# Scores and transposes of every second attention step behind the next group of products

## The reference

```
# layer 0: pooling mixer on 768 columns + memory attention (4 heads of 64) on 256
# layer 1: dilated window attention (12 heads: 3 groups, (window, dilation) =
#          (128,1), (512,4), (2048,16)) + memory attention
z = rms_norm(x, g) @ w_in[l]
s = einsum(q, k) * 64**-0.5          # per head; masked to a band for dilated attention
p = exp(s - logsumexp(s))
o = einsum(p, v)
# dilated groups: o weighted by softmax over the groups' logsumexp
x = x + rms_norm(concat(y_main, y_mem) @ w_out[l], g1)
h = rms_norm(x, g2); x = x + rms_norm((silu(h@wg) * (h@wu)) @ w_down[l], g3)
# after layer 0: shared keys and values, kv = rms_norm(x) @ w_kv, rotary on k
```

## Time and profile before

| | before |
|---|---|
| median of 3 runs | 2105.54 us (2105.05 to 2107.71) |
| the profiled execution: time, span | 2110.79 us, 2109.0 us |
| mean granted TensorE clock | 0.985 of full |
| TensorE busy | 2003.6 us, 95% |
| VectorE, ScalarE, GpSimd busy | 1466.9, 938.2, 340.2 us |
| TensorE waiting for ACT before scores (L869) | 32.5 us in 27 waits |
| TensorE waiting before transposes (L880) for ACT's copy of PO | 15.7 us in 17 waits |
| TensorE waiting before value products (L848) | 8.6 us in 9 waits |

### The profile page before, as it was taken

One profiled execution on the slowest core, in us unless ns is written; L12 is line 12 of the kernel. 1 busy time (PEld: TensorE's weight loads), 2 busy tenths in 40 slices (PEclk: granted clock), 3 DMA queues, 4 the chain that ended last, 5 costly groups with the idle time before them and its releaser, 6 DMA issues. The chain is left out here.

```text
span 2109.0 us, 25437 instructions
## 1 busy us (share of the span) xinstructions
PE 2003.6 (95%) x9458; PEld 1608.6 (76%) x9458; DVE 1466.9 (70%) x2080; ACT 938.2 (44%) x1514; POOL 340.2 (16%) x188
## 2 busy tenths in 40 slices
PE   7997999999999999999999986899999999999997
PEld 6765788888888888887766664578788888887886
DVE  6567676576788866575455565677879988885665
ACT  6345353455545444433455556656522222234341
POOL 3643000111212000000000051030123333310001
PEclk9999999999999999999999998999999999999998
DMA  4228741365687876484221100114246654477644
GB/s 173 97 71 312 260 144 41 132 228 209 235 295 278 332 273 210 171 290 166 71 69 62 61 21 21 51 61 134 86 162 244 236 191 152 173 279 265 204 162 157
DMA packets 119899, 357.37 MB, mean 169 GB/s; under 512 B 10848, under 2 KB 12256, under 8 KB 114528
## 3 DMA queue, kind: packets, MB, share of 16 engines
q1 hardware_dynamic: 103312, 325.59, 43.3%
q10 hardware_dynamic: 16464, 30.15, 4.1%
HBM read 241.28 MB, written 114.43 MB: 169 GB/s over the span
## 5 line engine op out<-in xcount | busy, mean ns | idle before, releaser
L981 PE MATMUL PS<-RP,DH 128*128 128x512 f32 x616 | 241.2, 392 | 1.7 <-DVE RP L2215 1.7
L982 PE MATMUL PS<-RP,DH 128*128 128x512 f32 x616 | 240.4, 390 | 0.0
L983 PE MATMUL PS<-RP,DL 128*128 128x512 f32 x616 | 240.3, 390 | 0.0
L963 PE MATMUL PS<-BHT,SH 128*128 128x512 f32 x576 | 224.1, 389 | 0.0
L964 PE MATMUL PS<-BLT,SH 128*128 128x512 f32 x576 | 224.1, 389 | 0.0
L965 PE MATMUL PS<-BHT,SL 128*128 128x512 f32 x576 | 224.1, 389 | 0.0
L963 PE MATMUL PS<-BH,SH 128*128 128x512 f32 x432 | 168.2, 389 | 0.6 <-DVE SL L2116 0.6
L965 PE MATMUL PS<-BH,SL 128*128 128x512 f32 x432 | 168.1, 389 | 0.0
L964 PE MATMUL PS<-BL,SH 128*128 128x512 f32 x432 | 168.1, 389 | 0.0
L981 PEld LDWEIGHTS PS<-RP,DH 128*128 128x128 f32 x616 | 116.0, 188 | 27.0 <-DVE RP L2215 3.1
L1098 ACT ACTIVATE DH<-DR 128x1408 fp32r<-128x1408 f32 x56 | 77.2, 1379 | 131.9 <-DMA DR<-s_keep 85.5
(11 more groups left out here) (331 smaller groups left out, 4734.5 us busy)
## 6 DMA issues: line engine op xcount, KB each, us to landing
SR<-in_wst SPq DMA_DIRECT2D x36, 1024.0 KB, 5.0
ZS<-in_wdn SPq DMA_DIRECT2D x32, 704.0 KB, 5.8
s_keep<-ZS SPq DMA_DIRECT2D x32, 704.0 KB, 4.7
DR<-s_keep SPq DMA_DIRECT2D x32, 704.0 KB, 5.2
inner<-TP SPq DMA_DIRECT2D x36, 512.0 KB, 4.2
WR<-in_w SPq DMA_DIRECT2D x35, 512.0 KB, 4.9
DR<-in_wdn SPq DMA_DIRECT2D x24, 704.0 KB, 5.1
RR<-t_keep SPq DMA_DIRECT2D x16, 1024.0 KB, 5.3
```

The lines of the kernel that those rows point to most:

```text
L963: MM(BANK[bank], SH[b][:, w, c], BH[t][:, k, :], start=(k == 0), stop=False)
L981: MM(bank, wh[:, i, :], rh, start=(i == 0), stop=False)
L982: MM(bank, wh[:, i, :], rl, start=False, stop=False)
L983: ins = MM(bank, wl[:, i, :], rh, start=False, stop=(i == KD - 1))
```

## The change

On TensorE an even step that is called from a job's hook issues only its value products (and lse rows, where it has them) at once. Its scores and transposes are put into a function `rest`, which the next hook runs first (`flush`), so behind the next group of products of the job. If the step stands at a job's last hook, that group is the first of the next job. Odd steps, and steps outside hooks (in the pooling jobs), stay whole. Nothing is changed on the other engines. Line numbers below L829 move by 7 to 20: L848, L869 and L880 become L855, L880 and L891.

```diff
--- before.py
+++ after.py
@@ -829,8 +829,15 @@
                                               LX[:, n, :, :].rearrange("p h c -> p (h c)"), IDENT)
                 ins.then_inc(px_full, 1)
 
-            def step(_=None):
-
+            def flush():
+
+                if att.get("rest"):
+                    rest, att["rest"] = att["rest"], None
+                    rest()
+
+            def step(later=False):
+
+                flush()
                 a, end = att["PE"], A_END if att.get("second") else A_END0
                 begin = 0 if end == A_END0 else A_END0
                 att["PE"] += 1
@@ -849,36 +856,45 @@
                                      start=(i == 0), stop=(i == nk // P - 1))
                             if i == nk // P - 1:
                                 ins.then_inc(pv_done, 1)
-                if a < end and a % 2 == 0:
-                    sl, kind, l, t, _h, n, k0, nk, _m = tile_of(a)
...
-                if begin <= a - 2 < end:
-                    b = a - 2
...
+
+
+                def rest():
+
+                    if a < end and a % 2 == 0:
+                        sl, kind, l, t, _h, n, k0, nk, _m = tile_of(a)
...
+                        if a:
+                            pe.wait_ge(exp_done, a)
+                        for h in range(2):
...
+                            MM(score_bank(a + h)[:, 0:nk], QF[rows, t, P * n:P * (n + 1)], keys,
+                               start=True, stop=True).then_inc(scored, 1)
+                    if begin <= a - 2 < end:
+                        b = a - 2
+                        l, nk = tile_of(b)[2], tile_of(b)[7]
+                        pe.wait_ge(p_normed, b + 1)
+                        if b:
+                            pe.wait_ge(pt_done, b)
+                        if b % 4 == 0 and b > begin:
+                            pe.wait_ge(o_free, b // 4)
...
+                        ins.then_inc(p_tr, 1)
+
+                if later and a % 2 == 0:
+                    att["rest"] = rest
+                else:
+                    rest()
                 if end == A_END and (a - 3) % 16 in (0, 3):
                     sl, r = (a - 3) // 16 - 1, (a - 3) % 16 // 3
                     if 3 <= sl <= 8:
@@ -886,8 +902,9 @@
 
             def steps_at(places):
                 def hook(i):
+                    flush()
                     if i in places:
-                        step()
+                        step(True)
                 return hook
 
             def first_ready(k):
```

More of the change, by code:

```diff
@@ L871, in step @@
-                if begin <= a - 2 < end:
-                    b = a - 2
[L873 to L881, removed]
+                def rest():
+                    if a < end and a % 2 == 0:
+                        sl, kind, l, t, _h, n, k0, nk, _m = tile_of(a)
+                        if a % 16 == 0:
+                            if kind == "mem":
+                                pe.wait_ge(*read_out(J[("in", l, t, None if l == 0 else 1)]))
+                                pe.wait_ge(mem_scaled, 4 * l + 4)
+                                pe.wait_ge(px_free, px_order["PE"].index(("mv", l)) + 1)
+                                if a == 0:
+                                    pe.wait_ge(*read_out(J[("in", 0, POOL_IN[0], None)]))
+                            else:
+                                pe.wait_ge(roped, 2 * (sl - 3) + 2)
+                                pe.wait_ge(px_free, px_order["PE"].index(("v", sl - 3, 1)) + 1)
+                        if a:
+                            pe.wait_ge(exp_done, a)
+                        for h in range(2):
+                            rows = slice(DH * h, DH * (h + 1))
+                            keys = KM[rows, t - NMT, :] if kind == "mem" else KF[(sl - 3) % 2][rows, k0:k0 + nk]
+                            MM(score_bank(a + h)[:, 0:nk], QF[rows, t, P * n:P * (n + 1)], keys,
[8 more added lines that the diff above has]
+                            pe.wait_ge(o_free, b // 4)
+                        for i in range(nk // P):
+                            ins = nc.tensor.transpose(PTR[:, P * i:P * (i + 1)], PR[l][:, b % 2, P * i:P * (i + 1)], IDENT)
+                        ins.then_inc(p_tr, 1)
```

## The result

The changed kernel takes 2127.39 us (median of 5 runs, 2124.09 to 2136.21), the kernel before 2107.71 (5 runs, 2105.05 to 2113.06). The ratio is 1.0096, 95% interval 1.0080 to 1.0111: slower, by 19.7 us on the medians. The forecast of slower by 7.2 us had the sign and missed the size, and its range ended at 2120. The profiled execution took 2128.43 us with a span of 2126.6, at a mean granted clock of 0.986 (0.985 before).

A forecast was written before the change was run, and what follows sets the result against it. TensorE, busy 95% of the span, was taken as the bound, so order could only change its idle time. The terms 2.6 + 5.8 + 4.4 - 3.8 - 1.8 gave +7.2 us on 2105.54: 2112.7 us, range 2101 to 2120.

The forecast's parts named there:

- Breaks: Further passages between products and small matmuls at 74 deferred steps: 0.035 us each, +2.6 us, between 1.5 and 5.9.
- The end of the value jobs: Five deferred steps at last hooks move behind the next job's wait for bank copies: +5.8 us, between 0 and 10.5.
- the fifth end: Job end before 1267.78 us: about 0.1 us, as VectorE's L2513, held by GpSimd, would end at the same time.
- The output jobs: 1284 to 1350 us, 8 waits before value products: a group (0.46) and a break (0.09) added to each, +4.4 us.
- the first stretch: 65 to 190 us: some five of seven waits before scores shrink where VectorE is held by other work, -1.8 us.
- the ring: Attention's chain of scores, maximum, exponential, normalisation, transposes, copy, value products; said to set the pace from 1284 to 1350 us.
- The covered waits: 15 waits before transposes for ScalarE's output copy, 13.1 us, are filled by the group of products: -3.8 us taken.
- the second stretch: 1030 to 1400 us, where attention steps stand between projection products; holds 66 of the 78 deferred steps.
- Neutral: Rival: the ring only turns by a group and spills at job ends find slack on VectorE: 2105.5 us, chance 0.27.
- faster: Rival: all 15 waits for the output copy are covered, the spill at job ends costs half: 2099.2 us, chance 0.15.
- The clock: Rival: longer stalls drop TensorE's clock at four or five more lengthened waits: +6, 2118.7 us, chance 0.13.

The follow-up runs named there:

- experiments 2 and 3: Kernel before plus 56 batches of value-like and score-like matmuls in layer 1's down projections, in one row or one group of products apart: 2230.64 and 2236.74 us.
- mid_jobs: The change, but steps at a projection job's last hook and in the output jobs stay whole: 2114.80 us, ratio 1.0030.
- mid_whole: Kernel before, with whole even steps (value products, scores, transposes together) one group later, only in the middle of projection jobs: 2110.32 us, ratio 1.0002.
- whole_later: Kernel before, with every even step called from a hook moved whole behind the next group of products: 2122.10 us, ratio 1.0072.
- no_spill: The change, but steps at a projection job's last hook stay whole: 2121.13 us, ratio 1.0061.
- spill_only: The change with only the five steps at a value job's last hook cut, all others whole: 2118.71 us, ratio 1.0058.
- out_only: The change without its part in the 18 projecting jobs of layer 1: 2115.15 us, ratio 1.0037.
- out_whole: The change, but all steps in the output jobs stay whole: 2127.19 us, ratio 1.0086.
- extra_apart: Kernel before plus 56 batches of value-like and score-like matmuls in layer 1's down projections, with a group of three products between the kinds: 2236.74 us.

## Why the forecast had the sign and not the size

**Breaks (forecast +2.6).** This is the step that failed, and the largest of the misses. The prediction took the 0.15 us between eight value products at 0.055 and the 0.59 they need for "the passage into the scores" and let it vanish when the two are parted. It doesn't: the last value product takes 0.20 us to whatever follows. It was a residue of the working, not a price seen at a change of neighbours. The pieces that were right, 0.08 back to products and 0.09 into small matmuls, then stand alone, and the break costs 0.20 (experiments 2 and 3), not 0.035. The timelines hold 73 further breaks (10, then 63; behind the last of the 74 value rows nothing is left to part): 14.6 us gross. The prediction's own upper end of 0.08 each, 5.9 us, was too low by the same error. For the 46 to 48 in the middle of jobs the net is 5.9 to 6.3 us (mid_jobs against mid_whole and against before). For the whole change the net is smaller than the gross, since a break that falls into a wait shortens it: whole_later, with the delays and no break, is only 5.3 us faster than the change.
The Trainium skill ("TensorE: Matmul & The Clock Gate", LDWEIGHTS (loading the stationary operand)) has a load of 128 weight columns take 107 ns. The prediction's estimate from it, one such load a break, was dismissed since products pace at 0.23 us. It comes closer than my 0.035, but the trace has nearly twice as much, 0.20, on two sides of the group, and no run here shows that weight loads are the reason.

**The end of the value jobs (+5.8).** Right in mechanism: new waits of the first product for ACT TP at 1052.93, 1108.10, 1161.75, 1212.79 and 1273.21 of the change, 7.2 us, and waits of lse rows behind DVE's rotary work. In the company of the other parts they are worth 6.3 us (change against no_spill). By themselves they cost 12.0, of which 6.8 in the waits, against 5.8 forecast. Wrong was the fifth end: 0.1 us, because DVE would be held up by POOL anyway. In spill_only DVE's two operations there start later against POOL's and take 2.72 and 2.86 us, 5.6 together, as before (1.54 and 4.04), so the delay is passed on: 0.8 us of wait and a break.

**The output jobs (+4.4).** no_spill against mid_jobs gives 6.3; out_only gives 6.6, with the breaks of the first stretch in it. Right in sign; the group in the ring was counted, but with a break of 0.09 instead of 0.20, and only at the 8 waits. Left out, and so put at nothing, was a wait of the steps that stay: an odd step's transposes need ScalarE's copy of the deferred ones (`pt_done`), which now comes a group later while they don't move. By the starts the odd transposes' waits are 29 and 12.2 us in the change, 16 and 9.3 us in out_only, against 4 and 1.6 us before; two of them in each, 1.5 to 1.7 us, are for VectorE. The profile's idle times show less than half of the 12.2. The longest of the value products' waits, on TensorE's timeline after:

```profile
1309.96 0.44 PE L855 MATMUL PTR<-PT,VF 128*64 128x128 f32 x4 [1.78 <-ACT PT L1226]
```

The PT waits before value products grew, as forecast, from 7.2 to 9.4 us.

**The covered waits (-3.8) and the first stretch (-1.8).** The waits shrank as forecast and more (OF 13.1 to 6.1 us; first stretch 9.2 to 6.3). But hardly any time is won. The first stretch got 0.5 us shorter in the change; but it took 119.64 us in spill_only, which has the instructions of before there, and 120.24 in out_only, which has those of the change. So single executions differ by more than the 1.8 forecast, and a gain of that size is neither shown nor excluded. In the second, mid_jobs shows where it goes. Its waits for OF fell from 13.1 to 7.5 and those before scores from 22.2 to 15.3 us, 12.5 together. New are lse rows 5.3, job starts 3.3, value products 1.1, PX 1.2, and 2.0 by the starts before odd transposes: 12.9. Nothing is left of the cover.

**The sum.** Added in this order the parts are mid-jobs 6.3, output jobs 6.3, value jobs' ends 6.3: 18.9 of 19.7 us. Forecast for the same three: some 2.6 - 3.8 - 1.8, 4.4 and 5.8. So 9.3 of the 12.5 us missed lie in the first: breaks too cheap, and covers counted as gains. In another order the three come out otherwise (see below), so I also add up each profiled stretch: the further breaks of the second stretch, counted as further places where TensorE leaves products, by 0.20 us; the change of all its waits by the profile; and the change of the part of the odd transposes' waits that the profile doesn't show.

| kernel | breaks x 0.20 | waits | hidden | sum | stretch, against 402.6 |
|---|---|---|---|---|---|
| the change | 63: 12.6 | -0.1 | 6.6 | 19.1 | +19.0 |
| out_whole | 44: 8.8 | 4.3 | 2.4 | 15.5 | +16.0 |
| no_spill | 57: 11.4 | -3.8 | 5.7 | 13.3 | +12.7 |
| out_only | 19: 3.8 | -2.2 | 3.9 | 5.5 | +4.6 |
| mid_jobs | 38: 7.6 | -1.1 | 2.0 | 8.5 | +6.2 |
| mid_whole | 2: 0.4 | -1.4 | 2.4 | 1.4 | +1.2 |
| whole_later | 2: 0.4 | 3.9 | 6.2 | 10.5 | +12.8 |
| spill_only | 6: 1.2 | 4.2 | 0.2 | 5.6 | +8.8 |

The rest is within 1 us but for three kernels, and there the clock lost in the stretch differs from before in the same direction (-3.4, +5.1 and +3.4 us; the change has +3.4 and needs none of it). These are single executions, so the sum is a check and no proof. It says that of the change's 19 us some 12.6 are breaks and some 6.6 the hidden waits, while gains and losses in the waits that the profile shows cancel.

**The rivals.** Neutral and faster fall. But neutral had the covers right: in mid_jobs the waits only changed their names. Faster had the OF waits covered (7.0 of its 10 us), and still no gain. The clock: the profile after has 3.4 us more of lost clock than before by the sum above, little more than half of the +6 of that rival. One fall lies at the fifth end, in the windows' row after (columns as in the earlier trace rows):

```profile
1270.00:1280.00 10.00, 7.62 (x27) 5.14 (x26) 4.62 (x7) 4.79 (x11) 8.88 (x4) 0.66 0.16 54
```

**What stays open.** By the medians the parts don't add: ends and mid-jobs together are +18.7 (out_whole), and the output jobs on top add 0.2, not 6.3. By the ratios it is 2.1 us, against 6.5 from mid_jobs to no_spill, and each has some 4 us of uncertainty, so even that isn't clear of noise. The stretches tell more. From the output jobs' first product to the last value products it is 102.4 us before:

```profile
1284.36 0.47 PE L724 MATMUL PS<-CH,WH 128*128 128x512 f32 x1
```

and 110.8 in the change:

```profile
1295.30 0.50 PE L724 MATMUL PS<-CH,WH 128*128 128x512 f32 x1
```

It is 104.7 in out_whole, 102.4 in mid_jobs, 108.0 in no_spill and 108.5 in out_only. So cutting the output jobs costs the same in each pair: 6.1 (change and out_whole), 5.6 (no_spill and mid_jobs), 6.1 (out_only and before). What differs is ahead of them, where both kernels have the same instructions: up to there out_whole took 313.9 us and the change 310.7. The two profiles part at the fifth end. In the change:

```profile
1269.82 7.03 POOL L2724 TENSOR_TENSOR OF<-OF,MX 128x1024 f32<-128x1024 f32 x3 [3.96 <-ACT MX L1666]
...
1276.48 1.45 DVE L2531 TENSOR_TENSOR TP<-TP,SIN 128x1024 f32<-128x1024 f32 x1
1277.96 2.03 DVE L2534 TENSOR_TENSOR KF<-TP,TP 128x1024 f32<-128x1024 f32 x1
1277.97 4.42 POOL L2655 TENSOR_TENSOR WL<-WR,WH 128x512 fp32r<-128x512 f32 x2 [1.12 <-ACT WH L1119]
...
1283.31 0.66 PE L828 MATMUL PX<-CN,LX 128*128 128x128 f32 x4 [1.21 <-DVE LX L1943]
```

and in out_whole:

```profile
1271.05 7.10 POOL L2724 TENSOR_TENSOR OF<-OF,MX 128x1024 f32<-128x1024 f32 x3 [4.09 <-ACT MX L1666]
...
1276.53 2.70 DVE L2531 TENSOR_TENSOR TP<-TP,SIN 128x1024 f32<-128x1024 f32 x1
1278.11 5.14 POOL L2655 TENSOR_TENSOR WL<-WR,WH 128x512 fp32r<-128x512 f32 x2
1279.27 2.84 DVE L2534 TENSOR_TENSOR KF<-TP,TP 128x1024 f32<-128x1024 f32 x1
...
1285.26 1.11 PE L828 MATMUL PX<-CN,LX 128*128 128x128 f32 x4 [4.81 <-DVE LX L1943]
```

In the change DVE's first operation (1.45 us) starts as POOL's three end (1276.85), and its second (2.03) starts just ahead of POOL's next (L2655). In out_whole POOL's three started 1.2 us later: the first (2.70) starts 1.6 us before they end, the second (2.84) in the midst of POOL's next, and the lse rows wait 3.6 us longer. What moved the two engines against each other I can't tell. The granted clock falls near there in both (0.66 from 1270 to 1280 in the change, 0.57 from 1267 to 1271 in out_whole). That is one execution of each, so whether it is the rule isn't shown.

## What to carry to other kernels

Put a row of small matmuls into a stream of products once, not twice: each further visit costs its entry and its return, busy time that no wait shows and that no idle time elsewhere pays for unless it falls into that wait. A wait of an engine that is busy for 95% may be covered and still give nothing, if the ring that made it only turns a group further: look whether the stage's length, not the wait's row, would shrink. Ask of every instruction that stays where it was whether it needs the result of one that moves: its wait grows by what the other is late. And a step at the end of a job covers the next job's start; take it out, and what it covered is paid twice, at the start and behind the next step's chain.

## What the runs showed of the hardware that was not expected

A change from 128x512 products to score matmuls costs 0.10 us beyond their own time, back from value or score matmuls 0.11, back from transposes 0.09, into transposes less than 0.01 (medians of starts; 0.200 us a further break in extra_apart). The last value product of a row takes 0.20 us to its follower, whichever it is. Idle time ahead of a small matmul behind a product is understated by 0.16 us, since the product's modelled end overlaps: 29 waits of the odd transposes sum to 12.2 us by their starts. And DVE's rotary operations, 1.22 and 2.00 us by themselves, took 2.70 and 2.84 where they started in the midst of a POOL operation (4.04 in the earlier trace rows). Started 0.01 us ahead of POOL's two (L2655) the second took 2.03, and those two took 4.42 us, where one by itself takes 1.27. So the cost of a delay there depends on where POOL stands.
